# Hybrid trunk step on one core: one convolution tile on TensorE, expert 0's first rows among the lists, probabilities scaled by VectorE

## The reference, cut to what matters

```python
def conformer_conv(u, conv_w, conv_b, ln_g, ln_b):
    val, gate = jnp.split(u, 2, axis=-1)
    g = val * jax.nn.sigmoid(gate)
    h = depthwise_conv(g, conv_w, conv_b, C_CONV // 2, C_CONV // 2)
    return jax.nn.silu(layer_norm(h, ln_g, ln_b))

...
s = jnp.einsum('bqhgd,bkhd->bhgqk', qblk, k) * scale
p = jax.nn.softmax(s, axis=-1)
o = jnp.einsum('bhgqk,bkhd->bqhgd', p, v)

...
logits = (h @ w_router) + b_router
top_v, top_i = lax.top_k(logits, TOP_K)
```

## Time and profile before

| | share of the span or value |
|---|---|
| PE busy | 1704.5 us, 88% |
| DVE busy | 1332.5 us, 69% |
| ACT busy | 805.0 us, 42% |
| POOL busy | 284.7 us, 15% |
| chain that ended last: PE | 75% |
| chain: DVE | 12% |
| chain: ACT | 5% |
| chain: issue | 5% |
| chain: DMA | 3% |

### The profile page before, as it was taken

How to read it: one execution, slowest core, us unless ns; L and a number is a source line. 1 busy time by engine, 2 the same in 40 slices (tenths; PEclk the granted TensorE clock), 3 DMA queues, 4 the chain that set the end, 5 groups by cost and what they waited for, 6 DMA issues and landing times.

```text
span 1937.8 us, 32671 instructions
## 1 busy us (share of the span) xinstructions
PE 1704.5 (88%) x11239; PEld 1560.4 (81%) x11240; DVE 1332.5 (69%) x2402; ACT 805.0 (42%) x1297; POOL 284.7 (15%) x280
## 2 busy tenths in 40 slices
PE   6896799999999999997377896599999999999992
PEld 4893599999999999994143494399999898999991
DVE  3778746658878886468887256545787888875446
ACT  3426343222122222323356535234764677754331
POOL 2001100000000000019950000100220122111012
PEclk9997899999999999997589998799999999999996
DMA  9443224437754443521000012145995999967334
GB/s 277 154 150 118 79 76 138 124 107 228 232 175 131 124 143 93 146 66 44 3 0 1 1 44 105 45 118 169 290 308 186 289 333 337 328 198 226 112 98 170
DMA packets 312658, 288.89 MB, mean 149 GB/s; under 512 B 20874, under 2 KB 301802, under 8 KB 312468
## 3 DMA queue, kind: packets, MB, share of 16 engines
q1 hardware_dynamic: 299012, 251.90, 42.1%
q0 software_dynamic: 12272, 34.23, 5.5%
q10 hardware_dynamic: 1184, 0.51, 0.1%
HBM read 263.38 MB, written 23.20 MB: 148 GB/s over the span
## 4 chain that ended last, share of the span: by engine, by line
PE 75%; DVE 12%; issue 5%; ACT 5%; DMA 3%; DVEq 0%; POOL 0%; SPq 0%; ACTq 0%; POOLq 0%
PE ps L1355 19%; PE ps L1356 19%; PE ps L1357 19%; PE ps L1360 6%; PE ps L1361 3%; DVE vp L2467 1%; DVE lo L2091 1%; PE ps L1418 1%; PE ps L1689 1%; ACT hi L833 1%; DMA raw<-in_moe_w_dram 1%; PE ps L1468 1%; DVE hot L2707 1%; DMA xrows<-in_x_sample_dram 1%; PE ps L1677 1%
## 5 line engine op out<-in xcount | busy, mean ns | idle before, releaser
L833 ACT ACTIVATE hi<-raw 128x1024 fp32r<-128x1024 f32 (+3 forms) x442 | 395.7, 919 | 509.9 <-PE ps L1357 436.3
L2091 DVE TENSOR_TENSOR lo<-raw,hi 128x1024 fp32r<-128x1024 f32 (+3 forms) x442 | 458.4, 1057 | 173.8 <-ACT hi L833 168.3
L1355 PE MATMUL ps<-h_wide,hi 128*128 128x320 f32 (+2 forms) x1728 | 539.2, 312 | 10.8 <-DVE h_wide L2189 5.4
L1357 PE MATMUL ps<-h_wide,lo 128*128 128x320 f32 (+2 forms) x1728 | 534.7, 309 | 0.0
L1356 PE MATMUL ps<-h_wide,hi 128*128 128x320 f32 (+2 forms) x1728 | 534.7, 309 | 0.0
L1355 PEld LDWEIGHTS ps<-h_wide,hi 128*128 128x128 f32 x1728 | 327.7, 190 | 13.9 <-issue 10.7
L1356 PEld LDWEIGHTS ps<-h_wide,hi 128*128 128x128 f32 x1728 | 327.4, 189 | 0.4 <-issue 0.2
L1357 PEld LDWEIGHTS ps<-h_wide,lo 128*128 128x128 f32 x1728 | 327.3, 189 | 0.0
L1355 PE MATMUL ps<-g_both,hi 128*128 128x320 f32 (+1 forms) x528 | 164.2, 311 | 2.6 <-DVE g_both L2406 2.6
L1356 PE MATMUL ps<-g_both,hi 128*128 128x320 f32 (+1 forms) x528 | 162.2, 307 | 0.0
L1357 PE MATMUL ps<-g_both,lo 128*128 128x320 f32 (+1 forms) x528 | 162.2, 307 | 0.0
(11 more groups left out here) (387 smaller groups left out, 2755.0 us busy)
## 6 DMA issues: line engine op xcount, KB each, us to landing
raw<-in_moe_w_dram SPq DMA_DIRECT2D x160, 512.0 KB, 5.8
raw<-in_w_mod_dram SPq DMA_DIRECT2D x96, 512.0 KB, 4.7
raw<-in_moe_w_dram SPq DMA_DIRECT2D x96, 384.0 KB, 4.1
raw<-in_ff_w_dram SPq DMA_DIRECT2D x40, 512.0 KB, 4.7
raw<-in_moe_w_dram SPq DMA_DIRECT2D x64, 256.0 KB, 3.6
y_rows<-zeros POOLq DMA_DIRECT2D x22, 512.0 KB, 4.4
raw<-in_ev_w_in_dram SPq DMA_DIRECT2D x12, 512.0 KB, 8.0
raw<-in_ff_w_dram SPq DMA_DIRECT2D x16, 384.0 KB, 3.6
```

Of the source, the lines that this page charges most:

```text
L833: act.activation(hi[c % 2][:, parts[h]], raw[slot][:, parts[h]], ACT.Copy).then_inc(hi_done, 1)
L1355: pe.matmul(out, w_hi, v_hi, start=first, stop=False, skip_group_check=True)
L1357: return pe.matmul(out, w_lo, v_hi, start=False, stop=last, skip_group_check=True)
L2091: dve.tensor_tensor(lo[c % 2][:, parts[h]], raw[ring_of(c) % 4][:, parts[h]], hi[c % 2][:, parts[h]].bitcast(F32), ALU.subtract).then_inc( ...
```

## The change

Three things change.

1. Convolution tile 3 leaves POOL. POOL now writes 31 diagonal matrices of 128x128, one for each tap (`diag(j)`, in a part of `h_wide` that is free once the projections are out: it waits for `evac` at 2 * OOUT). PE multiplies them with shifted windows of the gated input, 512 columns into bank 7 and 128 into bank 2, in groups: 3 pairs before the head sums, 5 before the spread, 3 behind each of four swaps, and the last 11 behind the final swap. ACT adds the bias on the way out, after the high parts of the keys and before the first exponentials, and PE waits for that (`c_kept`) before the scores of step 1. `spread` moves to banks 0, 1, 3 and 4 and now waits for `v_kept`.
2. The scaling of the probabilities moves from ACT (`normed` is gone) to DVE, behind the reciprocal, and the probabilities get a third buffer (`probs(s)`, in `tmp[:, 3]`): the exponentials of step s wait for the transposes of step s-3. 25 of DVE's own taps move ahead of attention: before it stand 55 in place of 30 (28 in place of 22 among the projections, 10 in place of 4 before the reciprocal step, 9 in the rotary loop, 4 in the loop that splits the queries), and each attention step has one tap in place of two.
3. The making of the lists moves, in program order on PE, ACT and DVE, to where expert 0's rows are turned, and its products and transposes get other PSUM places (banks 0, 1, 4, 5), so that banks 2, 3, 6 and 7 are free for the rows. Behind list product 5 PE loads the table of expert 0 and turns the first two tiles; ACT takes their high parts behind its copy 5 and DVE their low parts behind list 7. The third tile follows after the lists. A product of list e now also waits for `r_ids` at e - 1.

```diff
+        DIAG_HIGH = 20
+        diag_high = place("diag_high", [P, DIAG_HIGH, P], at=at_hh + 16 * HW)
+        diag_low = place("diag_low", [P, C_CONV - DIAG_HIGH, P], at=at_hl + 16 * HW)
+
+        def diag(j):
+
+            return diag_high[:, j, :] if j < DIAG_HIGH else diag_low[:, j - DIAG_HIGH, :]
+
+        def probs(s):
+
+            return tmp[:, 3, 0:T] if s % 3 == 2 else pp[:, s % 3, :]
...
+        FIRST_ROWS = 5
+
+        def tiles_first(eng, size, tile):
+
+            tile(0)
+            with eng.If(holds(size, 2)):
+                tile(1)
+
+        def tiles_more(eng, size, tile):
+
...
+            act.wait_ge(c_conv, 1)
+            act.activation(vp[:, NC - 1, GC_S - 15:GC_S - 15 + TS], ps[:, 7, 0:TS], ACT.Identity, bias=par[:, 1, CCB + NC - 1:CCB + NC])
+            act.activation(vp[:, NC - 1, 0:TP], ps[:, 2, 0:TP], ACT.Identity, bias=par[:, 1, CCB + NC - 1:CCB + NC]).then_inc(c_kept, 1)
+
...
-            def normed(s):
-
-                width = P if s % TT == 0 else T
-                act.wait_ge(a_sum, s + 1)
-                act.activation(pp[:, s % 2, 0:width], pp[:, s % 2, 0:width], ACT.Copy, scale=am[:, 3, s % 2:s % 2 + 1]).then_inc(a_norm, 1)
...
-                    if s >= 2:
-                        act.wait_ge(a_t, s - 1)
+                    if s >= 3:
+                        act.wait_ge(a_t, s - 2)
...
-                if 1 <= s < NH * TT + 1:
-                    normed(s - 1)
                 if 2 <= s < NH * TT + 2:
                     kept(s - 2)
...
+            for e in range(NE):
+                act.wait_ge(r_info, e + 1)
+                if e:
+                    act.wait_ge(r_info_turned, e)
+                act.activation(info_t[:, :].rearrange("p (h t) -> p h t", h=2), ps[0:4, 4 * (e % 2):2 + 4 * (e % 2), 0:TH],
+                               ACT.Copy).then_inc(r_info_kept, 1)
+                if e == FIRST_ROWS:
+                    act.wait_ge(r_tables, 1)
+                    gather(0, tiles_first)
+            gather(0, tiles_more)
...
+            def conv(n):
+
+                for j in range(taps_done[0], taps_done[0] + n):
+                    pe.wait_ge(diag_set, j + 1)
+                    pe.matmul(ps[:, 7, 0:TS], diag(j), gp[:, NC - 1, GC_S - 15 + j:GC_S - 15 + j + TS], start=j == 0, stop=j == C_CONV - 1,
+                              skip_group_check=True)
+                    last = pe.matmul(ps[:, 2, 0:TP], diag(j), gp[:, NC - 1, j:j + TP], start=j == 0, stop=j == C_CONV - 1,
+                                     skip_group_check=True)
+                    if j == C_CONV - 1:
+                        last.then_inc(c_conv, 1)
+                taps_done[0] += n
...
             pe.wait_ge(evac, 2 * OOUT)
             pe.wait_ge(odd_in, 16 * 6)
+            pe.wait_ge(gp_set, NC)
+            conv(3)
             for i in range(5):
...
+            conv(5)
             pe.wait_ge(o_rs, 1)
+            pe.wait_ge(v_kept, 1)
...
-                    last = pe.matmul(ps[:, 2 * (i % 2) + h, 0:TH], hspread[:, i, :], hrs[:, h * TH:(h + 1) * TH],
+                    last = pe.matmul(ps[:, 3 * (i % 2) + h, 0:TH], hspread[:, i, :], hrs[:, h * TH:(h + 1) * TH],
...
                 spread(i)
                 if i >= 1:
                     swap(i - 1)
+                    conv(3)
 
             swap(4)
             pe.transpose(ps[:, 5, 2 * P:3 * P], kf[:, 0:P], ident).then_inc(v_turned, 1)
+            conv(C_CONV - taps_done[0])
 
...
+                    if s == 1:
+                        pe.wait_ge(c_kept, 1)
...
-            pe.wait_ge(c_pool, 1)
...
+            pe.wait_ge(ht_kept, 2 * TT)
+            for e in range(NE + 1):
+                if e < NE:
+                    pe.wait_ge(r_hot, e + 1)
+                    if e >= 2:
+                        pe.wait_ge(r_info_kept, e - 1)
+                        pe.wait_ge(r_ids, e - 1)
+                    for h in range(2):
+                        for t in range(TT):
+                            last = pe.matmul(ps[0:4, 4 * (e % 2) + h, 0:TH], tok_w[:, t, e, :], hot[e % 2][:, t, h * TH:(h + 1) * TH],
+                                             start=t == 0, stop=t == TT - 1)
+                    last.then_inc(r_info, 1)
+                if e:
+                    pe.wait_ge(r_info_kept, e)
+                    for g in range(TT):
+                        last = pe.transpose(ps[:, 1 + 4 * ((e - 1) % 2), 384 + 4 * g:384 + 4 * g + 4], info_t[:, g * P:(g + 1) * P], ident[0:4, 0:4])
+                    last.then_inc(r_info_turned, 1)
+                if e == FIRST_ROWS:
+                    pe.wait_ge(r_tables, 1)
+                    load_tables(0)
+                    gather_first(next_size(), next_before())
+
             pe.reg_mov(expert_now, 0)
             first_marks = {}
             mark_next(pe, next_size(), first_marks)
-            gather_first(next_size(), next_before())
             gather_more(next_size(), next_before())
             wait_apart(pe, g_lo_kept, pe.value_load(tiles_after[0:1, 0:1], min_val=1, max_val=NE * TT))
-            pe.wait_ge(mats_in, 16)
+            pe.wait_ge(r_ids, NE)
...
-                    taps((4, 7, 4, 7, 0)[p - 2])
-
-            taps(4)
+                    taps((5, 9, 5, 9, 0)[p - 2])
+
+            taps(10)
...
                 qn(i)
                 if i:
                     rope(i - 1)
+                    taps(3 if i == 1 else 2)
...
                 dve.tensor_tensor(q_tall[HEADS[1], j, TP:T], qf[HEADS[0], j, TP:T], q_keep[HEADS[0], :].bitcast(F32), ALU.subtract).then_inc(q_lo, 1)
+                taps(1)
...
                     dve.reciprocal(am[:, 3, u % 2:u % 2 + 1], am[:, 2, u % 2:u % 2 + 1]).then_inc(a_sum, 1)
+                    dve.wait_ge(a_sum, u + 1)
+                    width = P if u % TT == 0 else T
+                    dve.tensor_scalar(probs(u)[:, 0:width], probs(u)[:, 0:width], am[:, 3, u % 2:u % 2 + 1], None, ALU.mult).then_inc(a_norm, 1)
                 if s >= 12 and (s - 2) % TT == 0:
                     head_lo((s - 12) // TT)
-                taps(2)
+                taps(1)
             taps(len(todo))
...
-            gather(0)
...
+                if e >= 2:
+                    info(e - 2)
+                if e == FIRST_ROWS + 2:
+                    gather(0, tiles_first)
+            for e in range(NE - 2, NE):
+                info(e)
+            gather(0, tiles_more)
...
-            pool.wait_ge(gp_set, NC)
             pool.wait_ge(par_kept, 1)
...
+            pool.wait_ge(evac, 2 * OOUT)
             for j in range(C_CONV):
-                w = par[:, 2, NC * j + c:NC * j + c + 1]
-                if j == 0:
-                    pool.tensor_scalar(vp[:, c, 0:conv_w], gp[:, c, 0:conv_w], w, par[:, 1, CCB + c:CCB + c + 1], ALU.mult, ALU.add).then_inc(pchain, 1)
-                else:
-                    pool.tensor_scalar(tmp[:, 3, 0:conv_w], gp[:, c, j:j + conv_w], w, None, ALU.mult).then_inc(pchain, 1)
-                    pool.wait_ge(pchain, 2 * j)
-                    ins = pool.tensor_tensor(vp[:, c, 0:conv_w], vp[:, c, 0:conv_w], tmp[:, 3, 0:conv_w], ALU.add)
-                    ins.then_inc(c_pool if j == C_CONV - 1 else pchain, 1)
-                    if j < C_CONV - 1:
-                        pool.wait_ge(pchain, 2 * j + 1)
+                pool.tensor_scalar(diag(j), ident, par[:, 2, NC * j + NC - 1:NC * j + NC], None, ALU.mult).then_inc(diag_set, 1)
```

87 lines of the change are left out of this document (31 added, 56 removed).

## The result

The changed kernel takes 1911.84 us in the median (1908.60 to 1915.12) beside 1939.65 us (1938.46 to 1945.14) for the kernel before on the same chip: a ratio of 0.9853, interval 0.9827 to 0.9878, that is 27.8 us. The forecast was 1911.5 us. The profiled execution, the slowest of the four, took 1915.12 us with a span of 1913.2, 24.6 us under the span before.

The account below looks back on a forecast made before the run. It took the prelude as a chain of small steps, attention's start as DVE's queue, later heads as a loop of waits. Terms -3, -10.5, -11.5 and -3.5 sum to -28.5, giving 1911.5 us; range 1896 to 1930.

Parts of the forecast that it names:

- The rival of half clock: Prelude: PE stays at half clock despite the pairs, prelude +42 us, total 1956 us; chance 0.08.
- PE's side in sum: Prelude: the 31 tap pairs on PE at full clock, less what faster sums and spreads give back, cost +3 us.
- The first three pairs: Prelude, before the head sums: pairs mostly fill PE's idle time, +1 us, or +5 at half clock.
- a factor of 0.66: Prelude: DVE's tap takes 1341 ns beside POOL, 891 without; applied to DVE's path instructions, 5 us saved (bounds 0 and 8).
- the step of 2.6 us: Attention's start: each of 12 steps falls to the later loop's 2.6 us, giving 33.2 us, a saving of 10.5.
- The scaling's price: Attention steps on DVE: scaling taken at 0.47 us from the list comparison, making DVE's step 2.35; at 0.82 it is 2.70.
- the 2.56 of the sum: Later heads: a two-step loop from scores through exponentials and transposes takes 5.11 us, or 2.56 a step.
- the 16.26: Later heads: us per head before the change, forecast to fall to 14.4, saving 11.5 us over six heads.
- DVE as the bound: Attention: scaling at 0.82 us and doubled waits make a step 2.9 to 3.0 us, total 1922.5; chance 0.14.
- PE's own pace: Later attention loop closes at PE's 2.37 us a step, heads of 13.4, total 1896 us; chance 0.10.
- the third buffer does nothing: Attention: the single place for transposes orders steps anyway, 3.1 us a step, total 1929 us; chance 0.04.
- the 3.65 of the earlier trace: Expert 0's rows: the last stretch to the first expert product, kept at 3.65 us in a forecast saving of 3.5.

Follow-up runs that it names:

- second profile of after: The changed kernel, nothing altered, run and profiled once more beside later kernels: 1910.8 us, 0.9847 of the kernel before.
- before with POOL silent: The kernel before with 30 of POOL's 31 taps for tile 3 left out, read only up to the layer norm sums: 1911.9 us, 0.9847.
- the edit to the low part: Changed kernel with the low part of a head's output ahead of reciprocal and scaling on DVE, and PE's branch marks earlier: 1903.3 us, 0.9817.
- the best kernels of this study: Changed kernel with the head output's low part first, plus PE's table loads and marks before the list loop (1901.8 us), or two pairs a swap round (1902.1 us).

## Why the prediction was right, and where it was not

**The prelude's clock: right.** It is 1.00 over the swaps (0.91 in the second profile of after), rounds are 5.57 us against 5.6, and taking away the pairs brings 0.50 back. The rival of half clock had its cause right, since the stretch without pairs stays at 0.50, but the pairs decide as I argued. PE's side in sum: the prelude of after is 3.9 us longer than that of before with POOL silent, against +3; the matrices and the earlier taps are in that too. The first three pairs were priced at 1 us and cost 2.9: PE waits 2.95 us for the first matrix, and the head sums begin 8.1 us behind the last projection in place of 5.2 or 5.3.

**POOL's silence: mis-sized.** I took 5 us from a factor of 0.66 that the long taps show and put the upper bound at 8. It measured 9.5. The short instructions on the path shrink by half or more: the four q_wide 2.9 us, the four k_low 2.5, the four q_tall 1.7; the additions of the rotation, 1626 against 692 ns, weren't in my sum at all. A factor from one form was carried to another, where the price is a wait for POOL's running instruction. The matrices cost POOL 31.68 us for 31, 1.02 each, against 0.45; all but the first hid, since PE waits for no other in the prelude.

**The start: right in kind, 3.8 us too small.** Two things were at work, as forecast: the silence (4.5 us, with nothing else changed) and one tap a step. What was mis-sized is the step of 2.6 us that I took from the later loop although I wrote that no product with the values stands in it before step 7. With that loop gone, DVE's list is what is left (DVE is busy 25.95 of 29.39 us), and it was in my text with 2.35 us. Timeline of DVE of after, two steps in the start:

```profile
967.35 0.82 DVE L2606 TENSOR_REDUCE am<-ps 128x1 f32<-128x640 f32 x1 [0.93 <-DVE vp L2512]
968.09 0.15 DVE L2612 RECIPROCAL am<-am 128x1 f32<-128x1 f32 x1
968.28 0.55 DVE L2615 TENSOR_SCALAR pp<-pp,am 128x640 f32<-128x640 f32 x1
968.74 0.90 DVE L2514 SCALAR_TENSOR_TENSOR vp<-gp,par,vp 128x655 f32<-128x655 f32 x1
969.68 0.82 DVE L2606 TENSOR_REDUCE am<-ps 128x1 f32<-128x640 f32 x1
```

969.68 - 967.35 = 2.33 us, and 12 of them with the head's end, 2.0, are 30.0, an estimate, against 29.4 measured. The scaling's price, taken from the lists' comparison with 0.47 us to the next instruction, is exact: 968.28 to 968.74, 0.46.

**The six heads: the loop right, the clock not foreseen.** At full clock the turns of one head come after 2.74, 2.33, 2.37, 2.74 and 4.16 us, 14.34 in all against 14.4 forecast; the mean of the first four, 2.55, is the 2.56 of the sum without its rounding. But three of the six heads ran at 0.89 and took 16.0 us, 4.7 us more in all, and the last head, behind which no scores follow, took 12.2, 2.2 less. The earlier trace rows had 0.93 for these heads before, and the heads before are 17.1 us where the clock is 0.90 and 15.7 at 1.00; I carried the 16.26 as if it were one number and priced only the full clock. From full clock to full clock a head gains 1.2 to 1.4 us, not 1.9. The 1.7 us more at the end of attention have the same cause, a clock of 0.84 from 1068.5 to 1079 us; in most of the other profiles it is 4.6 us as before.

**The rivals.** DVE as the bound is what happens with the 25 taps back; with one tap it isn't in the later heads, as DVE is busy 62.0 of 89.0 us. PE's own pace, heads of 13.4, is not reached by the change but nearly by the edit to the low part (13.7). That the third buffer does nothing is true of the later heads only because the scaling has left ACT: it is worth 4.4 us in the start, part of it perhaps clock, and without both the old loop is back.

**The rows: 1.1 us short.** The lists end 144.1 us behind the layer norm sums, 4.0 later than before (5.6 forecast). Behind them stand 10.3 us, not 7.6: I took the 3.65 of the earlier trace rows for the way into the expert code over unchanged, and it became 8.07. A second profile of after has 2.1 us less in this stretch, so the 1.1 us are within what one profile can tell; the 4.4 us more of the way in aren't, as no profile with the new order is under 6.7.

**The sum.** The prelude and the start gave 6.4 us more than forecast; the heads, the end of attention, the rows and the projection's end 6.9 less. That the total came within half a microsecond of the forecast's difference is in good part luck: single terms were off by up to 4.7 us, and the expert loop, in which nothing was forecast, moved by 3.4.

## What to carry to other kernels

A wait loop through several instructions can be opened at any link, so undo the links singly and together before you call one of them worthless, and compare stretches at the same granted clock. When one engine leaves a shared path, price each instruction on the other engine by its own row with and without the neighbour, since what it loses was a wait for the neighbour's instruction and not a fixed share of its length. Put what the next stage waits for (here the low part of a head's output) at the head of its engine's queue, before work that has slack: 8.2 us in six heads here for two moved lines, more than half of it clock, and it is why the best kernels of this study, at 1901.8 and 1902.1 us, are 0.9796 of the kernel before.

## What the runs showed of the hardware that I had not expected

- PE busy for 17.4 of 20 us with spreads of 10 rows and swaps keeps a granted clock of 0.50; with two or three fp32 pairs of 128 rows to a round it is 0.91 to 1.00.
- With PE busy for all of 8.4 us at 1.00, the clock fell to 0.50 at the end of eight spreads of 10 rows, and stayed there over the swaps and spreads that followed.
- The addition of the rotation, two SBUF inputs, took 1626 ns in the mean beside POOL (0.69 us or 1.94) and 692 without it; an instruction with one PSUM input took 881 and 883.
- POOL's product of a 128x128 matrix with a column took 1.02 us in the mean, 0.45 of what 655 columns took the earlier trace rows.
- PE's way from the last turned tile to the first expert product was 3.65 us in one order of the code and 6.7 to 8.6 in another, with the table loads and marks out of it in one of them; in every profile of the second order a 16 KB packet of an instruction queue ended 1.7 to 2.1 us ahead of that product.
